# Two transformer blocks on one core: square passes on four quarters, output tiles between states, and a gate folded into the last weights

## The reference

```
# first block
h = rms_norm(x); mem_h = rms_norm(mem)                 # mem: 256 rows
c_glu, c_gate, d_q, d_k, d_v, d_gate, x_q, x_gate, merge = split(h @ w_in)
y_conv = (silu(layer_norm(conv31(a * sigmoid(b)))) * silu(c_gate)) @ w_conv_proj
y_diff = differential_attention(8 heads) * silu(d_gate) @ w_diff_proj
k, v   = split(mem_h @ w_mem_kv); k = rms_norm(k) per head; q = rms_norm(x_q)
y_mem  = (softmax(q k^T / 16) v * silu(x_gate)) @ w_x_proj      # 4 heads of 256
x = x + (sum over branches of sigmoid(merge_i) * y_i) @ w_out
# second block
x = layer_norm(x, emb)
sh1, sc1, gt1, sh2, sc2, gt2 = split(silu(c) @ w_ada + b_ada)
p = (x * (1 + sc1) + sh1) @ w_in_2
y_a = gelu(pu) * (tril(w_s) applied to layer_norm(gelu(pv)) in chunks of 128)
y_b = rwkv7_time_mix(p): per token and head (8 heads of 64)
      S = S * w + (S a) b^T + v k^T;  y = S r;  then group norm, bonus, gate
x = layer_norm(ALPHA * x + gt1 * (concat(y_a, y_b) @ w_out_2), ln1)
g, u = split((x * (1 + sc2) + sh2) @ w_ffn_in)                  # 2816 each
x = layer_norm(ALPHA * x + gt2 * ((silu(g) * u) @ w_ffn_out), ln2)
```

## Time and profile before

| | |
|---|---|
| median of 3 runs | 1738.71 us (1736.97 to 1738.91) |
| profiled execution, its own time | 1738.34 us |
| its span | 1736.6 us |
| mean granted TensorE clock | 0.978 of full |
| busy: TensorE, VectorE, ScalarE, GpSimd | 1627.2, 1003.6, 723.5, 192.7 us |
| weight loads of TensorE (beside its matmuls) | 1283.6 us |
| DMA | 166.07 MB, mean 96 GB/s |

### The profile page before, as it was taken

One profiled execution on the slowest core, in us unless ns is written; L12 is line 12 of the kernel. 1 busy time (PEld: TensorE's weight loads), 2 busy tenths in 40 slices (PEclk: granted clock), 3 DMA queues, 4 the chain that ended last, 5 costly groups with the idle time before them and its releaser, 6 DMA issues. The chain is left out here.

```text
span 1736.6 us, 24246 instructions
## 1 busy us (share of the span) xinstructions
PE 1627.2 (94%) x9944; PEld 1283.6 (74%) x9944; DVE 1003.6 (58%) x1644; ACT 723.5 (42%) x1145; POOL 192.7 (11%) x158
## 2 busy tenths in 40 slices
PE   6999989999999999899999899999888999999995
PEld 5777776788787766677788686788666887887883
DVE  5999976666655476566444647675437443332227
ACT  5543346344522476467522635553325222222111
POOL 2343335400010000000005000000000000000000
PEclk9999999999999999999999999999989999999998
DMA  5222323654465322221333232200012332222321
GB/s 199 97 85 74 97 85 121 199 178 145 137 181 154 98 79 72 79 91 61 122 97 117 86 103 73 73 4 4 3 37 75 107 118 88 91 92 85 97 73 48
DMA packets 45644, 166.07 MB, mean 96 GB/s; under 512 B 5264, under 2 KB 5392, under 8 KB 45536
## 3 DMA queue, kind: packets, MB, share of 16 engines
q1 hardware_dynamic: 42912, 155.95, 28.0%
q0 software_dynamic: 2624, 8.59, 1.6%
HBM read 162.42 MB, written 2.10 MB: 95 GB/s over the span
## 5 line engine op out<-in xcount | busy, mean ns | idle before, releaser
L607 DVE TENSOR_TENSOR weight_lo<-raw,weight_hi 128x1024 fp32r<-128x1024 f32 x184 | 225.6, 1226 | 487.7 <-ACT weight_hi L599 487.7
L564 PE MATMUL bank<-h_T_hi,weight_hi 128*128 128x512 f32 x1208 | 496.3, 411 | 5.5 <-DVE h_T_lo L1998 3.4
L599 ACT ACTIVATE weight_hi<-raw 128x1024 fp32r<-128x1024 f32 x241 | 254.5, 1056 | 569.9 <-PE bank L566 567.2
L565 PE MATMUL bank<-h_T_lo,weight_hi 128*128 128x512 f32 x1208 | 480.2, 397 | 0.0
L566 PE MATMUL bank<-h_T_hi,weight_lo 128*128 128x512 f32 x1208 | 479.9, 397 | 0.0
L564 PEld LDWEIGHTS bank<-h_T_hi,weight_hi 128*128 128x128 f32 x1208 | 229.0, 190 | 70.7 <-issue 11.6
L565 PEld LDWEIGHTS bank<-h_T_lo,weight_hi 128*128 128x128 f32 x1208 | 228.8, 189 | 55.6 <-issue 5.6
L566 PEld LDWEIGHTS bank<-h_T_hi,weight_lo 128*128 128x128 f32 x1208 | 228.6, 189 | 55.2
L1993 DVE SCALAR_TENSOR_TENSOR bank<-conv_in,columns,bank 128x512 f32<-128x512 f32 x240 | 181.4, 756 | 8.3
L607 POOL TENSOR_TENSOR weight_lo<-raw,weight_hi 128x1024 fp32r<-128x1024 f32 x57 | 141.3, 2485 | 205.5 <-ACT weight_hi L599 205.5
L566 PE MATMUL bank<-branch_hi,weight_lo 128*128 128x512 f32 x192 | 75.9, 396 | 0.0
(11 more groups left out here) (442 smaller groups left out, 2324.2 us busy)
## 6 DMA issues: line engine op xcount, KB each, us to landing
raw<-in_weights SPq DMA_DIRECT2D x289, 512.0 KB, 3.5
x_in<-in_x SPq DMA_DIRECT2D x4, 512.0 KB, 5.4
x_rows<-in_x POOLq DMA_DIRECT2D x4, 512.0 KB, 4.9
out<-x_rows SPq DMA_DIRECT2D x4, 512.0 KB, 2.6
mem_in<-in_mem POOLq DMA_DIRECT2D x2, 512.0 KB, 8.0
ln_rows<-in_ln_g POOLq DMA_DIRECT2D x4, 256.0 KB, 3.9
ln_rows<-in_ln_b POOLq DMA_DIRECT2D x4, 256.0 KB, 4.5
silu_row<-in_c POOLq DMA_DIRECT2D x1, 512.0 KB, 11.0
```

The source lines that it names most:

```text
L564: pe.matmul(o, lhs[0], rhs[0], start=start, stop=False)
L565: pe.matmul(o, lhs[0], rhs[1], start=False, stop=False)
L599: act.activation(parts[n % SPLIT][0][:, :], raw[u % RAW][:, :], ACT.Copy).then_inc(*weight_hi.up(u))
L607: engine.tensor_tensor(lo[:, :], raw[u % RAW][:, :], view(hi[:, :]), ALU.subtract).then_inc(*ready.up(u))
```

## The change

Nine edits in one kernel:

1. *Keys.* `key_places` gets bank 1 as a third place, and the normed keys stay in their PSUM bank, where `key_hi` and `dve_key_lo` read them. `value_places` go 0, 5, 1, 4.
2. *Silu loop.* `silu_ring` becomes PSUM banks 6 and 7 (two places), and the inverse root of the convolution is written into the bank of its mean. In `gated(n)` the rest of feature n-1 comes before `normed(n+2)`.
3. *Cross head 0.* `x_gate` 0 comes first, before the two `xq` units. The `ada` units: `proj` 0 had a second one behind every odd unit, four in all; these four now stand behind `d_gate` of every second differential head.
4. *Chunk levels.* `pe_level` alternates the matmuls of X and Y, the second into the other half of the lanes, with rows crossed or turned from level to level so that every output lies where the next level reads it. A level of X and Y is one step.
5. *States and output.* States 2 and 3 use the ring `half_places` and are interleaved with the first three token units of `w_out_2`, one token tile at a step (`pe_out_steps`; ScalarE and VectorE feed at steps 4, 8 and 12), and `gate_rows(2)` comes after them.
6. *Row norms.* `bn_stats` of the first half of a row runs before the wait for its second half; `act_modulated` makes the product of feature k before it rounds feature k-1.
7. *Start of `ffn_out`.* `last_places` go 3, 4, 5, 6, 7, 0, 1, 2.
8. *Last weights.* VectorE multiplies each of the 22 raw `ffn_out` units with gt2 (`dve_scale`), in `feed_lo` before the split of the unit ahead of it; ScalarE makes the hi part behind that (`weight_scaled`).
9. *Tail.* A residual is one operation that also sums its row (ALPHA x + product); the mean from it, (x + mean) * gain, the variance by a Square with a sum on ScalarE, and one multiply-add with the inverse root and the bias. Of the last three units tile 0 is done unit by unit.

```
-    mem_places, key_places, key_sums = bank_ring((6, 7)), bank_ring((6, 7)), bank_ring((2,))
-    value_places, square_places = bank_ring((0, 1, 5, 4)), bank_ring((4,))
+    mem_places, key_places, key_sums = bank_ring((6, 7)), bank_ring((6, 7, 1)), bank_ring((2,))
+    value_places, square_places = bank_ring((0, 5, 1, 4)), bank_ring((4,))
+    conv_places, silu_ring = ..., ring([bank[:, :] for bank in banks[6:8]])
-    half_places, last_places = bank_ring((0, 1, 2, 3)), bank_ring(range(8))
+    half_places, last_places = bank_ring((0, 1, 2, 3)), bank_ring((3, 4, 5, 6, 7, 0, 1, 2))
...
# unit_plan
+        if h == 0:
+            for name, n in (("x_gate", 0), ("xq", 0), ("xq", 1), ("x_gate", 1)):
+                f((name, n), "w_in", W_IN_AT[name] + n * P)
...
             for d in range(KT):
                 f(("proj", 0, d), "w_conv_proj", d * P)
                 a()
-                if d % 2:
-                    a()
...
         f(("d_gate", h), "w_in", W_IN_AT["d_gate"] + h * P)
+        if h % 2 == 0:
+            a()
...
# dve_keys
-            mult(dve, conv[:, n, :], conv[:, n, :], conv_r_ring[0])...
+            mult(dve, conv[:, n, :], conv[:, n, :], stats["mean"])...
...
+            if n:
+                dve_branch_lo(dve, "conv", n - 1, silu_ring[n - 1])
             if n + 2 < KT:
                 normed(n + 2)
-            if n:
-                dve_branch_lo(dve, "conv", n - 1, silu_ring[n - 1])
...
+            if h == 0:
+                feature_unit(pe, ("x_gate", 0), unit_bank(pe, ("x_gate", 0)), h_T)
...
+    def pe_level(pe, banks, Y, V, table, crossed):
+        for m in range(8):
+            for part in range(2):
+                rows = cut(part ^ crossed, CHUNK)
+                x_done = pe_square(pe, banks[0], table(Y), table(V), m, rows, cut(part, CHUNK))
+                y_done = pe_square(pe, banks[1], table(V), table(Y), m, rows, cut(1 - part, CHUNK))
+        return x_done, y_done
...
# rwkv_rounds
+        interleave(states(2), states(3), out_steps())
         gate_rows(2)
-        interleave(states(2), states(3))
...
+    def pe_out_steps(pe):
+        pe.wait_ge(*ya_lo.at(TT - 1))
+        for pair in range(KT // 2 - 1):
+            if pair == 2:
+                pe.wait_ge(*yb_lo.at(1))
+            yield from token_steps(pe, ("w_out_2", 0), pair, first_out, (Mix(0), Mix(1)), ...)
...
# dve_rows
+            dve.wait_ge(*row_ready.at({"emb": "x1", "ln1": "x2"}[what], t, 0))
+            dve_piece_stat(dve, what, t, x_rows[t], 2, 0)
             dve.wait_ge(*residual(t))
-            dve_row_stat(dve, what, t, x_rows[t], 2)
+            dve_row_stat(dve, what, t, x_rows[t], 2, done=1)
...
# act_modulated
+        for k in features:
+            full = modulated_ring.take(...)
+            activate(act, full, turned_bank(what, g, k), ACT.Identity, bias=..., scale=...)
+            if k > features[0]:
+                rounded(k - 1)
+        rounded(features[-1])
...
# feed_hi
-            act.wait_ge(*raw_loaded[u % RAW].at(u))
+            act.wait_ge(*(weight_scaled.at(u) if plan[u][0][0] == "ffn_out" else raw_loaded[u % RAW].at(u)))
...
# feed_lo
+                if u + 1 < len(plan) and plan[u + 1][0][0] == "ffn_out":
+                    dve_scale(dve, u + 1)
                 if u not in by_pool:
                     split_lo(dve, u, weight_lo)
...
+    def dve_scale(dve, u):
+        dve.wait_ge(*raw_loaded[u % RAW].at(u))
+        for half in range(2):
+            dve.wait_ge(*gate_row.at(5, half))
+            slot = raw[u % RAW][:, cut(half, 512)]
+            done = dve.tensor_tensor(slot, slot, gate_tiles[5][half][:, :], ALU.mult)
+        done.then_inc(*weight_scaled.up(u))
...
# act_ffn
-            act_row_root(act, "ln2", t, EPS5)
+            mean, square = last_spots(t)
+            act.wait_ge(*last_mean.at(t))
+            activate(act, last_squares[:, :], x_rows[t][:, :], ACT.Square, bias=mean, accum=square)
+            act_root(...)
...
# dve_ffn
+    def dve_last_residual(dve, t, half):
+        dve.scalar_tensor_tensor(out=rows_half, in0=rows_half, scalar=ALPHA, in1=last_places["ffn", t, half],
+                                 op0=ALU.mult, op1=ALU.add, accum_out=sums[:, half:half + 1])
+    def dve_last_centred(dve, t):
+        dve.tensor_scalar(mean, sums[:, 0:1], sums[:, 1:2], -1.0 / D, ALU.add, ALU.mult)
+        for half in range(2):
+            fused(dve, o, x_rows[t][:, cut(half, 512)], mean, ln_rows[half][:, :], ALU.add, ALU.mult)
...
     def dve_last_rows(dve, t):
-        dve_row_norm(dve, "ln2", t, x_rows[t][:, :], row_ready.up("ln2", t))
...
+        for half in range(2):
+            fused(dve, x_rows[t][:, cut(half, 512)], final_ring["ffn", t, half], r, ln_rows[2 + half][:, :], ALU.mult, ALU.add)
```

More of the change, by code:

```diff
@@ L785, in token_unit @@
                 done.then_inc(*product.up(*label, "tile", t))
-        if not last:
-            done.then_inc(*product.up(*label, pair))
+            elif t == tiles - 1:
+                done.then_inc(*product.up(*label, pair))
+            yield
     def token_rows(pe, label, out_banks, lhs, turn):
@@ L1307, in pe_states @@
         for c in range(1, NC - 1):
-            bank = wide.take(pe, ("state", f, c), dve_s, f, "state", c)
+            bank = state_banks(f).take(pe, ("state", f, c), dve_s, f, "state", c)
             if c == 1:
@@ L1318, in pe_states @@
             yield
-        bank = wide.take(pe, ("later", f), dve_s, f, "later")
+        bank = state_banks(f).take(pe, ("later", f), dve_s, f, "later")
         pe.wait_ge(*dve_s.at(f, "state", NC - 2))
@@ L1327, in pe_states @@
         yield
-        bank = wide.take(pe, ("mean", f), dve_s, f, "centred")
+        bank = state_banks(f).take(pe, ("mean", f), dve_s, f, "centred")
         pe.wait_ge(*dve_s.at(f, "later"))
@@ L1335, in pe_states @@
         yield
-        bank = wide.take(pe, ("gate", f), dve_s, f, "y")
+        bank = state_banks(f).take(pe, ("gate", f), dve_s, f, "y")
         for n in range(2):
@@ L1628, in act_cross @@
             query_hi(h)
-            feed_hi(act)
-            gate(h, 0)
+            if later:
+                feed_hi(act)
+                gate(h, 0)
             if later:
@@ L2625, in dve_residual, with dve_out_steps @@
         return fused(dve, rows_half, rows_half, ALPHA, o, ALU.mult, ALU.add)
+    def dve_out_steps(dve):
+        dve_diagonals(dve, 2)
+        for n in range(3 * TT + 1):
+            if n in OUT_FEEDS:
+                feed_lo(dve)
+            yield
     def dve_second_out(dve):
```

226 lines of the change are left out of this document (134 added, 92 removed).

## The result

The changed kernel takes 1689.17 us (median of 4 runs, 1687.36 to 1690.89) where the kernel before took 1737.84 beside it: a ratio of 0.972, 95% interval 0.9703 to 0.9736, or 48.7 us. The prediction was 1685.0 with a range of 1675 to 1702. The profiled execution took 1690.89 us with a span of 1689.2, 47.4 less than the span of before.

The account below looks back on a forecast made before the run. TensorE, busy for 1627.2 of 1736.6 us, was taken to bound the kernel. Terms 5 + 12 + 15.5 + 5 + 4.4 + 11.8 = 53.7 us gave 1685.0 by the median, with a range of 8 in 10 from 1675 to 1702.

Parts of the forecast that it names:

- Keys: Key stage: the third place only moves TensorE's wait to POOL's split, with the unit starting at 249.6; 0.5 us lost.
- Silu loop: Loop before the first projection: with silu and r in PSUM, five VectorE operations no longer slow beside POOL; gain 5 us.
- rival (b): Silu loop: its two PSUM places and the wait of xq 1 tie it, the first stage gives nothing; 1690, chance 0.12.
- Chunk levels: Chunk stage: X and Y on four quarters overlap, a level's pair falls from 1.87 to 0.93 us; gain 12, bounds 0 and 15.
- Rival (a): Chunk levels: quarters don't overlap across banks, so the edit does nothing there; 1697, chance 0.12.
- States and output: Last states: twelve token tiles between the state steps fill TensorE's idle time; gain 15.5 us, bounds 10 and 17.5.
- Row norms: Two row norms: early statistic and products one feature ahead ready the last row sooner; gain 2.5 each, 5 us together.
- rival (c): Clock: its falls behind the row norms go too and the keys lose nothing; 1676, chance 0.15.
- Start of ffn_out: Last projection's start: beginning with banks 3 to 7 removes a bank wait (2.7) and the lower clock behind it (1.7); gain 4.4.
- Rival (d): Scaling of the last weights lands on the path, 92 us lost; net 1777, chance 0.03 with the like.
- Tail: VectorE's row work after the last matmul: fewer operations, 4.5 us a row instead of 7.7; gain 11.8, bounds 9 and 13.5.
- Rival (e): Whole kernel: several terms fall to their lower bounds together (10 + 3 + 2.7 + 9 + 6 + 0); 1708, chance 0.08.

Follow-up runs that it names:

- keys_in_sbuf: The changed kernel with the normed keys written to an SBUF tile again, the third key bank kept: 1696.01 us.
- silu_in_sbuf: The changed kernel with the silu tiles back in three SBUF places and the convolution's inverse root in an SBUF tile: 1697.81 us.
- after: The changed kernel itself, with all nine edits, timed beside the kernel before: 1689.17 us, ratio 0.972.
- same_quarters: The changed kernel with X and Y of a level still alternating, but both on the two diagonal quarters, no rows crossed or output turned: 1699.03 us.
- banks_in_order: The changed kernel with the banks of the last projection handed out from 0 to 7 again: 1693.64 us.
- no_scale: The changed kernel without the multiplication of the last weights by the gate, that factor left out of the computation: 1688.71 us.

## Why the prediction was right, and where its terms were off

The sum was 53.7 us; measured are 48.7 by the medians, 47.4 and 55.1 by the two pairs of traces. The mechanism was right for the silu loop, the levels, the start of `ffn_out`, the scaling and the tail, half right for the keys and the states, and wrong for the row norms. That the sum came so near is in part luck, for the misses had both signs.

- **Keys: -0.5 predicted, 2.1 to 3.0 measured.** The mechanism was right, the wait moves to POOL's split. The step that failed is "The mean of the convolution, behind half of it, comes no earlier". I had priced the slow operations of the silu loop, and not the two of the same kind in `dve_key_lo(0)`, 4.04 us together, which stand ahead of the taps. keys_in_sbuf shows it.
- **Silu loop: 5.5 predicted (5 with the keys' loss), 5.8 and 6.7 measured.** Every step held, down to the 1.45 us wait for `xq` 0's bank (1.4 predicted). silu_in_sbuf shows the cause. This rules out rival (b), as after does.
- **Chunk levels: 12 predicted, 8.1 and 9.8 measured.** The overlap is as priced; the stops of TensorE below had no term. Windows of the two stretches (columns as in the earlier trace rows), before, then after, and the waits that are new in after's timeline:

```profile
1135.40:1169.10 33.70, 33.68 (x942) 29.83 (x944) 24.39 (x42) 19.06 (x31) 0.00 (x0) 1.00 0.01 4
1169.20:1237.00 67.80, 66.56 (x1718) 56.39 (x1716) 34.54 (x67) 25.22 (x48) 0.00 (x0) 1.00 0.02 4
```

```profile
1128.60:1159.60 31.00, 27.21 (x942) 22.54 (x942) 24.10 (x41) 18.00 (x31) 0.00 (x0) 1.00 0.01 4
1159.60:1222.00 62.40, 58.85 (x1712) 48.36 (x1714) 34.80 (x68) 24.27 (x48) 0.00 (x0) 1.00 0.02 4
```

```profile
1131.78 0.24 PE L1211 MATMUL bank<-V,Y 64*64 64x64 f32 x1 [1.08 <-DVE LM0k L2077]
...
1156.67 0.97 PE L1211 MATMUL bank<-Y,V 64*64 64x64 f32 x26 [1.31 <-DVE V L2077]
...
1195.86 0.21 PE L1211 MATMUL bank<-Y,V 64*64 64x64 f32 x1 [1.39 <-issue]
...
1216.29 1.15 PE L1211 MATMUL bank<-AL,LM0a 64*64 64x64 f32 x32 [0.64 <-ACT AL L1992]
```

TensorE's busy time falls by 6.5 and 7.7 us, 14.2 of the 15 that I had as the bound. In the first pair 3.8 us of new idle time give part back: 1.08 and 1.31 us are waits for VectorE, 0.36 for ScalarE, and 1.02 (before 1139.02) a stop for which the profile names no releaser. 2.7 are left of the 4.5 that I counted. The 3 us that I took off for VectorE's work there were about right (2.75 with ScalarE's); the stop and the smaller fall of the busy time (6.5, not 7.5) are the rest. In the second, where I counted all 7.5, 0.64 us is a wait for ScalarE and 1.39 another such stop; 5.5 are left. The two stops stand inside levels, in both traces of after, and neither the kernel before nor same_quarters has them (see the last section). Rival (a) is out. The measured 0.99 us a level also goes against *TensorEngine Tiling (Array Packing)* of the Trainium skill, gotcha 1, in this form of matmul: alternating matmuls on different row tiles, two of the four quarters writing each bank, ran at twice the rate of two quarters.
- **States and output: 15.5 predicted, 14.9 and 15.5 measured.** The size is right, the reason was half of it: "puts twelve token tiles between the state steps" is worth 4.2 us by the traces, most of it a fall of the clock, and 5.2 by the medians; the rest comes from the y_a tiles no longer standing behind the wait for y_b.
- **Row norms: 5 predicted (bounds 3 and 10), 1 to 1.5 measured** (0.7 and 0.8 at the second norm; at the first the 4.20 us wait is 3.89, and what follows it varies by as much). The failed step is "moves ahead of the wait for the other half: 0.65 us a chain": at the second norm VectorE has no wait there, it comes late, and what moves ahead of the wait stays ahead of the row. In "every 0.66" the cadence is 0.76 us (a wait of 0.33 for ScalarE before each 0.43 us lo part), and the first lo part comes 0.3 us later for it. The falls of the clock behind both waits stayed, so rival (c) did not come.
- **Start of ffn_out: 4.4 predicted, 4.2 measured** in banks_in_order. The wait in the rows is 2.37 us and not the 2.7 of the sum. The stretch gained 5.5, with the 1.07 us wait for the last weight, which I had in the tail.
- **Scaling: 0 predicted, 0 measured** (no_scale). Rival (d) is out.
- **Tail: 11.8 predicted, 11.4 and that 1.1 measured.** No run takes this edit back alone; the number is that of the stretch, and how it divides among the merged operations is not shown. Windows of the last rows after (they answer to the earlier trace rows), and VectorE's timeline there:

```profile
1666.60:1686.10 19.50, 13.94 (x60) 10.87 (x58) 16.94 (x36) 8.24 (x17) 0.00 (x0) 0.94 0.20 81
1680.60:1686.10 5.50, 0.00 (x0) 0.00 (x0) 5.01 (x11) 1.74 (x4) 0.00 (x0) 0.79 0.23 95
```

```profile
1672.09 1.41 DVE L2080 SCALAR_TENSOR_TENSOR x_rows<-scratch,small,ln_rows 128x512 f32<-128x512 f32 x2 [1.10 <-ACT small L580]
...
1674.14 0.21 DVE L2781 TENSOR_SCALAR small<-small 128x1 f32<-128x1 f32 x1
...
1678.38 0.21 DVE L2781 TENSOR_SCALAR small<-small 128x1 f32<-128x1 f32 x1
...
1684.71 1.42 DVE L2080 SCALAR_TENSOR_TENSOR x_rows<-scratch,small,ln_rows 128x512 f32<-128x512 f32 x2 [0.42 <-ACT small L580]
```

A row takes 4.24 us (1674.14 to 1678.38; 4.5 predicted), row 0 is held back until 1672.09, 4.7 us behind its first product (5.0 predicted), and behind the last matmul VectorE works for 5.01 of 5.5 us instead of 16.42 of 17.0.

The miss of 5 us is the row norms (3.5 to 4) and the chunk levels (2 to 4), less what the keys gave beyond the forecast (3). In the norms I priced the edit at the wait and took VectorE's queue for free; in the levels 2.4 us of stops had no term.

Two numbers beside the sum don't come out of the working. Rival (e) takes 6 us for the levels and calls it their lower bound, which is 0. The scaling would decide from 8.0 us a unit, not 8.1 (53.7 / 22 is 2.4, above 5.6).

## What to carry to other kernels

Where an operation is slow for a reason (a port, a bank), look for every other operation of that kind before you sum; the two that I missed stood ahead of twelve taps. Moving work ahead of a wait gains nothing on an engine that arrives late at that wait: read its idle time there first. Where an edit makes small matmuls run twice as fast, allow for stops that no engine causes; here they took 2.4 us. And when a new order both interleaves work and lifts a wait, price the two apart; here the lifted wait was worth at least two and a half times the interleaving (10.7 us against 4.2).

## What the runs showed of the hardware

I summed, in windows of 1 us of each trace up to the last matmul, what the granted clock lacks to 1.0. Each fall takes off 1.7, 3.4 or 5.1 us, nothing between. The kernel before lacks 30.7 and 35.8 us so, the changed one 17.1 and 18.8, its variants 17.1 to 23.9. But part of this lies over idle time, where a low clock costs nothing: counted only while a matmul was running, the kernel before lacks 24.2 and 30.0 us and the changed one 16.0 and 15.9. So 8 to 14 us of the gain are the clock's, most of it behind waits that the edit shortened or took away. They are no term beside the others, but lie inside the stretches of the table. Which waits are followed by a fall differs between executions of the same code: behind the 3.05 us before the differential heads it fell in twelve of the fourteen traces, and the variants that leave the keys alone reach the values anywhere from 249.4 to 252.8 us. So a difference of a few us between two traces says nothing unless it is read between two events near each other.

TensorE also stops for 0.3 to 2.1 us at places where the profile names no releaser (`issue`), all in the chunk stage, with its small matmuls: five times in each trace of after, three times in each of the kernel before, and most of them at the same places of the code in every trace. The profile has a DMA queue of the kind "instruction"; its line on the page of after:

```profile
q8 instruction: 79, 1.29, 0.3%
```

These are 79 packets of 16 KB. In the chunk stage of after they come 3.4 to 8.9 us apart, elsewhere mostly 25 to 35. In the 14 traces there are 72 such stops (the 5 us that the kernel before waits for y_b aside), and every one begins between 0.7 us before and 1.1 us after the end of one of these packets; a moment taken at random in that stage does so in two of five cases. The stop that ends at 1195.86 begins at 1194.48, and the packet before it lands at 1194.36. That suggests that matmuls of 15 ns each use up their instructions faster than these are brought in, and it fits that same_quarters, whose levels take twice as long, has only three of the five stops. Most packets are followed by no stop, and no run varied the supply: the cause is not shown.
